# Recurrence of a two-layer block: inverses as plain products, level masks applied once per chunk

## The reference, cut to what matters

```
w = -softplus(-(w0 + tanh(wd) @ w2)) - 0.5 ; decay = exp(-exp(w))
a = sigmoid(a0 + ad @ a2)
kk = k * k_k, normed per head ; k = k * (1 + (a - 1) * k_a)
def step(state, (r, w, k, v, kk, a)):
    sa = state @ -kk
    state = state * w + outer(sa, kk * a) + outer(v, k)
    y = state @ r
```

## Time and profile before

| | |
|---|---|
| Median of 3 runs | 3220.7 us (3216.71 to 3222.69) |
| Span of the profiled execution | 3217.7 us; the page gives no other time of its own for it |
| Mean granted TensorE clock | 0.942 of full speed |
| Busy over the span | PE 88%, weight loads 71%, DVE 53%, ACT 30%, POOL 21% |

### The profile page before, as it was taken

The page is one execution under the profiler, slowest core; times in us unless marked ns, Lnnn a source line. Parts: engine busy times, 40 slices in busy tenths (PEclk is TensorE's granted clock), DMA queues, the critical chain, the costliest instruction groups (busy, mean ns, idle before and its releaser), DMA issues.

```text
span 3217.7 us, 49963 instructions
## 1 busy us (share of the span) xinstructions
PE 2847.2 (88%) x20746; PEld 2294.3 (71%) x20746; DVE 1695.8 (53%) x3047; ACT 978.0 (30%) x1832; POOL 676.8 (21%) x531
## 2 busy tenths in 40 slices
PE   7998878699999999869999977887878899999877
PEld 6776667588888888757788846777756678766655
DVE  3425565544444444576455227778745432377744
ACT  3214444311111111454221121222144222145552
POOL 2113233211101011063111102223202211122113
PEclk9998999899999999989999977989889899999988
DMA  3111032011111111113111200000032201111042
GB/s 99 50 54 45 14 100 73 25 59 46 46 49 50 46 53 40 46 53 105 53 34 46 76 21 2 3 29 3 3 99 79 87 32 35 34 40 37 30 127 95
DMA packets 200322, 162.45 MB, mean 50 GB/s; under 512 B 5232, under 2 KB 173850, under 8 KB 199586
## 3 DMA queue, kind: packets, MB, share of 16 engines
q1 hardware_dynamic: 200098, 159.26, 15.9%
HBM read 137.19 MB, written 22.05 MB: 49 GB/s over the span
## 4 chain that ended last, share of the span: by engine, by line
PE 72%; DVE 12%; ACT 6%; issue 5%; POOL 3%; DMA 2%; SPq 0%; DVEq 0%; ACTq 0%; POOLq 0%
PE ps L725 15%; PE ps L727 14%; PE ps L726 14%; PE ps L2291 7%; PE ps L1843 3%; PE ps L1767 2%; PE ps L1469 2%; PE ps L1471 1%; PE ps L1470 1%; ACT r L685 1%; PE ps L1834 1%; PE ps L777 1%; DVE r L690 1%; PE ps L779 1%; PE ps L778 1%
## 5 line engine op out<-in xcount | busy, mean ns | idle before, releaser
L725 PE MATMUL ps<-r,r 128*128 128x512 f32 (+1 forms) x2304 | 938.0, 407 | 96.8 <-DVE r L690 56.0
L726 PE MATMUL ps<-r,r 128*128 128x512 f32 (+1 forms) x2304 | 908.2, 394 | 0.0
L727 PE MATMUL ps<-r,r 128*128 128x512 f32 (+1 forms) x2304 | 907.7, 394 | 0.0
L725 PEld LDWEIGHTS ps<-r,r 128*128 128x128 f32 x2304 | 442.2, 192 | 229.6 <-DVE r L690 64.9
L671 POOL TENSOR_TENSOR sb<-sb 128x1024 f32<-128x1024 f32 x138 | 275.8, 2004 | 1301.8 <-DMA sb<-in_w_ffn_up 483.6
L726 PEld LDWEIGHTS ps<-r,r 128*128 128x128 f32 x2304 | 442.6, 192 | 93.7 <-issue 7.8
L727 PEld LDWEIGHTS ps<-r,r 128*128 128x128 f32 x2304 | 441.0, 191 | 94.0
L690 DVE TENSOR_TENSOR r<-sb,r 128x1024 fp32r<-128x1024 f32 x198 | 268.9, 1365 | 234.4 <-ACT r L685 234.1
L2291 PE MATMUL ps<-sb 64*64 64x64 f32 (+2 forms) x8832 | 298.6, 228 | 81.6 <-issue 47.8
L2291 PEld LDWEIGHTS ps<-sb 64*64 64x64 f32 (+1 forms) x8832 | 283.5, 138 | 106.7 <-issue 81.3
L685 ACT CAST r<-sb 128x1024 fp32r<-128x1024 f32 x198 | 204.9, 1043 | 215.9 <-POOL sb L671 215.8
(11 more groups left out here) (272 smaller groups left out, 3622.9 us busy)
## 6 DMA issues: line engine op xcount, KB each, us to landing
sb<-in_w_out SPq DMA_DIRECT2D x36, 512.0 KB, 4.1
sb<-in_a_w_in SPq DMA_DIRECT2D x29, 512.0 KB, 4.0
sb<-in_w_ffn_gate SPq DMA_DIRECT2D x22, 512.0 KB, 3.8
sb<-in_w_ffn_up SPq DMA_DIRECT2D x22, 512.0 KB, 3.9
sb<-in_w_ffn_down SPq DMA_DIRECT2D x22, 512.0 KB, 3.4
sb<-in_w_in SPq DMA_DIRECT2D x17, 512.0 KB, 4.1
sb<-in_x SPq DMA_DIRECT2D x16, 512.0 KB, 5.5
xs<-sb SPq DMA_DIRECT2D x4, 2048.0 KB, 9.7
```

What stands on the lines that cost most here:

```text
L725: pe.matmul(self.out, w.hi[:, q, self.cols], hi, start=(q == 0), stop=False)
L726: pe.matmul(self.out, w.hi[:, q, self.cols], lo, start=False, stop=False)
L727: ins = pe.matmul(self.out, w.lo[:, q, self.cols], hi, start=False, stop=(q == w.nk - 1))
```

## The change

The masks of the six levels become f16 constants, and DVE cuts L, copied to f16 by ACT, into its six levels once per chunk (`split_levels`). A level's W is then a plain product, and the sum with X becomes part of the products, since the identity is added to W by a further product in PSUM. What was a mask or a sum on DVE becomes a copy out of PSUM, half of them on ACT. `low`, `zi` and POOL's part go; the last correction is added in PSUM and ACT copies the result. The low-rank weights lie in one tile, w on the upper 64 rows and a on the lower, and their products alternate between both. The sigmoid's scaling moves into the constants of E: L2387 takes half of k_a, L2390 becomes (rate + 1) x kk, and L2400 a product with -0.5 in the same operation; L2322 goes. The order of a period is a new one, and the first three, partly empty periods take the place of the list ahead. The diff, cut:

```diff
@@ -160,8 +160,8 @@
-        self.level = [self.const(CH) for _ in range(6)]
-        self.level0t = self.const(CH)
+        self.masks16 = self.const(6 * CH // 2).bitcast(F16).rearrange("p (a b) -> p a b", a=6)
+        self.eye16 = self.const(CH // 2).bitcast(F16)
...
+    PERIOD = "S A S A L S A L S P P A B A P B P E B E A B B E A B E"
-        out = [("L", 0)] * 4 + [("E", 0)] * 4 + [("P", 0)] * 4 + [("E", 1)] * 4 + [("I", 0)] * 2 + [("L", 2)] * 4
-        out += [step for _ in range(4) for step in (("P", 1), ("I", 0))]
-        out += [step for _ in range(4) for step in (("I", 0), ("E", 2), ("I", 1))] + [("I", 0)] + [("I", 1)] + [("I", 0)] + [("I", 1)]
-        for m in range(NCH):
+        out = []
+        for m in range(-3, NCH):
             chunk = {"S": m, "A": m + 1, "P": m + 2, "B": m + 2, "E": m + 3, "L": m + 3}
-            for c in "S A S L A L L S L A S P P B E B E P P B A B B A E B A E".split():
-                if chunk[c] < NCH and (c != "L" or chunk[c] % 2 == 0):
+            for c in self.PERIOD.split():
+                if 0 <= chunk[c] < NCH and (c != "L" or chunk[c] % 2 == 0):
...
-                    ins = pe.matmul(self.bank(b + p // n, n, w)[o, p % n, :], lhs[o, p], rhs[o, p], start=(j == 0),
+                    ins = pe.matmul(self.bank(b + p // n, n, w)[o, p % n, :], lhs[o, p], rhs[o, p], start=(j == 0 and not onto and not (keep and p)),
...
     def low_rank_pe(self, pe, m):
         k, s = self.k, self.s
-        for dst, weights in (("tw", self.w2), ("ta", self.a2)):
-            for half, b in ((0, 0), (1, 1)):
-                pe.wait_ge(*self.freed(b))
-                for p in range(3):
+        for half in range(2):
+            pe.wait_ge(*self.freed(0))
+            pe.wait_ge(*self.freed(1))
+            for p in range(3):
+                for dst, b, o in (("tw", 0, slice(0, LORA)), ("ta", 1, slice(LORA, P))):
                     q = 3 * half + p
-                    ins = pe.matmul(self.bank(b, 3, 2 * CH)[:, p, :], weights[:, q * P:(q + 1) * P],
-                                    self.lora[:, m * CH:(m + 2) * CH], start=True, stop=True)
-                ins.then_inc(*s.low_rank.up((dst, m, half)))
-                k.free[b] = ("biased_" + dst, (m, half))
-                yield
...
                 dve.tensor_tensor(to[:, pairs], self.bank(b, 3, 2 * CH), over_tokens(bias[:, pairs], 2 * CH),
                                   ALU.add).then_inc(*s["biased_" + dst].up((m, half)))
-                if dst == "ta":
-                    dve.wait_ge(*s.tanh.at((dst, m, half)))
-                    dve.tensor_scalar(to[:, pairs], to[:, pairs], 0.5, 0.5, ALU.mult, ALU.add).then_inc(*s.rate.up((m, half)))
-                yield
...
-        b = 4 + 2 * (m % 2)
-        pe.wait_ge(*self.freed(b))
-        self.heads(pe, b, BT, CH, [(self.ar_e[:, :, 0, :], self.bb)]).then_inc(*s.p_low.up(m))
-        k.free[b] = ("low", m)
...
-        dve.wait_ge(*s.p_low.at(m))
-        dve.tensor_tensor(self.low[i], self.bank(4 + 2 * i), over_pairs(k.low), ALU.mult).then_inc(*s.low.up(m))
-        dve.wait_ge(*s.low.at(m))
-        dve.tensor_tensor(self.z[i], self.low[i], over_pairs(k.level[0]), ALU.mult).then_inc(*s.step_dve.up(("z", m)))
-        dve.wait_ge(*s.step_dve.at(("z", m)))
-        dve.tensor_tensor(self.x16[i], self.z[i], over_pairs(k.eye), ALU.add).then_inc(*s.inv_x.up((m, 0)))
+        dve.wait_ge(*s.inv_l.at(m))
+        self.split_levels(dve, m, 0, 1)
         dve.wait_ge(*s.p_ak.at(m))
         dve.tensor_tensor(self.ak[i][:, 0:3, :], self.bank(2, 3, 2 * CH), self.m3, ALU.mult)
         dve.tensor_tensor(self.ak[i][:, 3:6, :], self.bank(3, 3, 2 * CH), self.m3, ALU.mult).then_inc(*s.ak.up(m))
-        yield
-        yield
-        yield
-        yield
+        self.split_levels(dve, m, 1, 6)
+
+    def split_levels(self, dve, m, first, end):
+
+        shape = (P, end - first, BT, CH)
+        of_pair = self.l16.unsqueeze(1).broadcast_to(shape)
+        mask = self.k.masks16[:, first:end].unsqueeze(2).broadcast_to(shape)
+        dve.tensor_tensor(self.levels16[m % 2][:, first:end], of_pair, mask, ALU.mult).then_inc(*self.s.levels.up((m, first)))
...
-        if m > 1:
-            act.wait_ge(*s.inv.at(m - 2))
-        act.copy(self.l16[i], self.lr[i][:, :, 0:CH]).then_inc(*s.inv_l.up(m))
+        if m:
+            act.wait_ge(*s.levels.at((m - 1, 1)))
+        act.copy(self.l16, self.lr[i][:, :, 0:CH]).then_inc(*s.inv_l.up(m))
...
-        x16, xt16, w16 = self.x16[i], self.xt16[i], self.w16[i]
+        x16, xt16, w16, eyes = self.x16[i], self.xt16[i], self.w16[i], over_pairs(k.eye16)
+        level = [self.levels16[i][:, j] for j in range(6)]
+        pe.wait_ge(*s.levels.at((m, 0)))
+        pe.wait_ge(*self.freed(b))
+        self.heads(pe, b, BT, CH, [(level[0], eyes), (eyes, eyes)]).then_inc(*s.i_x.up((m, 0)))
+        pe.wait_ge(*self.freed(bt))
+        self.heads(pe, bt, BT, CH, [(eyes, level[0]), (eyes, eyes)]).then_inc(*s.i_xt.up((m, 0)))
+        k.free[b], k.free[bt] = ("inv_x", (m, 0)), ("inv_xt", (m, 0))
+        yield
         for lev in range(1, 6):
             if lev == 1:
-                pe.wait_ge(*s.inv_l.at(m))
+                pe.wait_ge(*s.levels.at((m, 1)))
             pe.wait_ge(*s.inv_x.at((m, lev - 1)))
             pe.wait_ge(*self.freed(b))
-            self.heads(pe, b, BT, CH, [(self.l16[i], x16)]).then_inc(*s.i_w.up((m, lev)))
+            self.heads(pe, b, BT, CH, [(level[lev], x16), (eyes, eyes)]).then_inc(*s.i_w.up((m, lev)))
             k.free[b] = ("inv_w", (m, lev))
             yield
             pe.wait_ge(*self.freed(bt))
             pe.wait_ge(*s.inv_w.at((m, lev)))
-            if lev == 1:
-                pe.wait_ge(*s.inv_xt0.at(m))
-            else:
-                pe.wait_ge(*s.inv_xt.at((m, lev - 1)))
+            pe.wait_ge(*s.inv_xt.at((m, lev - 1)))
             self.heads(pe, b, BT, CH, [(xt16, w16)]).then_inc(*s.i_x.up((m, lev)))
-            self.heads(pe, bt, BT, CH, [(w16, xt16)]).then_inc(*s.i_xt.up((m, lev)))
+            self.heads(pe, bt, BT, CH, [(w16, xt16)], keep=lev == 5).then_inc(*s.i_xt.up((m, lev)))
             k.free[b], k.free[bt] = ("inv_x", (m, lev)), ("inv_xt", (m, lev))
             yield
         pe.wait_ge(*self.freed(b))
-        pe.wait_ge(*s.inv_z.at(m))
-        self.heads(pe, b, BT, CH, [(self.low[i], self.z[i])]).then_inc(*s.i_rest.up(m))
+        pe.wait_ge(*s.inv_x.at((m, 5)))
+        self.heads(pe, b, BT, CH, [(self.lr[i][:, :, 0:CH], self.z[i]), (eyes, eyes)]).then_inc(*s.i_rest.up(m))
         k.free[b] = ("inv_rest", m)
         yield
-        pe.wait_ge(*self.freed(bt))
+        pe.wait_ge(*s.inv_xt.at((m, 5)))
         pe.wait_ge(*s.inv_rest.at(m))
-        self.heads(pe, bt, BT, CH, [(x16, self.r16[i])]).then_inc(*s.i_fix.up(m))
+        self.heads(pe, bt, BT, CH, [(self.r16[i], xt16)], onto=True).then_inc(*s.i_fix.up(m))
         k.free[bt] = ("inv", m)
...
-        k, s, i = self.k, self.s, m % 2
+        s, i = self.s, m % 2
         b, bt = 4 + 2 * i, 5 + 2 * i
-        x16, xt16, w16 = self.x16[i], self.xt16[i], self.w16[i]
+        dve.wait_ge(*s.i_x.at((m, 0)))
+        if m > 1:
+            dve.wait_ge(*s.i_fix.at(m - 2))
+        dve.tensor_copy(self.x16[i], self.bank(b)).then_inc(*s.inv_x.up((m, 0)))
+        yield
         for lev in range(1, 6):
-            dve.wait_ge(*s.i_w.at((m, lev)))
-            dve.tensor_tensor(w16, self.bank(b), over_pairs(k.level[lev]), ALU.mult).then_inc(*s.inv_w.up((m, lev)))
             yield
             dve.wait_ge(*s.i_x.at((m, lev)))
-            dve.tensor_tensor(x16, x16, self.bank(b), ALU.add).then_inc(*s.inv_x.up((m, lev)))
-            dve.wait_ge(*s.i_xt.at((m, lev)))
-            dve.tensor_tensor(xt16, xt16, self.bank(bt), ALU.add).then_inc(*s.inv_xt.up((m, lev)))
+            dve.tensor_copy(self.z[i] if lev == 5 else self.x16[i], self.bank(b)).then_inc(*s.inv_x.up((m, lev)))
             yield
         dve.wait_ge(*s.i_rest.at(m))
-        dve.wait_ge(*s.inv_zi.at(m))
-        dve.tensor_tensor(self.r16[i], self.bank(b), self.zi[i], ALU.subtract).then_inc(*s.inv_rest.up(m))
-        yield
-        dve.wait_ge(*s.i_fix.at(m))
-        if m > 1:
-            dve.wait_ge(*s.s_y.at(m - 2))
-        dve.tensor_tensor(self.xt[i], self.z[i], self.bank(bt), ALU.add).then_inc(*s.inv.up(m))
+        dve.tensor_tensor(self.r16[i], self.bank(b), self.z[i], ALU.subtract).then_inc(*s.inv_rest.up(m))
+        yield
         yield
...
-        for _ in range(10):
+        b, bt = 4 + 2 * i, 5 + 2 * i
+        act.wait_ge(*s.i_xt.at((m, 0)))
+        act.copy(self.xt16[i], self.bank(bt)).then_inc(*s.inv_xt.up((m, 0)))
+        yield
+        for lev in range(1, 6):
+            act.wait_ge(*s.i_w.at((m, lev)))
+            act.copy(self.w16[i], self.bank(b)).then_inc(*s.inv_w.up((m, lev)))
             yield
-        act.wait_ge(*s.inv_xt.at((m, 5)))
-        act.copy(self.z[i], self.xt16[i]).then_inc(*s.inv_z.up(m))
-        yield
-        yield
```

(76 more changed lines are left out.)

24 lines of the change are left out of this document (11 added, 13 removed).

## The result

The kernel after takes **3174.3 us** (median of 4 runs, 3172.24 to 3181.79) where the kernel before takes 3221.1: a ratio of 0.9861 [0.9847, 0.9875], 46.8 us less. The forecast was 3158. The profiled execution of after is its longest, 3181.79 us, and it reaches the recurrence late: the recurrence's first matmuls (L2253 in before, L2255 in after) start at 1905.1 us where before has 1895.2. So I compare stretches that begin there. From that point to the last state update it takes 414.3 us, and 460.4 before: 46.1 us, the whole difference of the medians.

What follows compares the result with a forecast made beforehand. DVE was taken to bound each chunk's second half, PE's products with ACT copies the first. Twelve periods 43 us, last three 6, start 12 and setup 1.8 made 62.8 us less: 3158 us, range 3134 to 3191.

Steps and rivals of the forecast that it cites:

- Start: Stretch ahead of the first state update: partly empty periods replace the old list, 12 us less, bounds 4 and 16.
- Last three: The last three periods, 60.4 us, hold no new products in part: 2 us less each, 6 in all.
- Setup: DVE's two memsets ahead of the w2 and a2 transfers, for which PE waits 7.49 us, go: 1.8 us less.
- (a): The 12 periods from 1987.9 to 2295.2 us: each falls from 25.6 to 22.0 us, 43 us in all.
- The first half: State matmuls of a chunk, PE products with ACT copies between: 8.1 us, 9.5 with low-rank part, mean 8.8 (9.3 before).
- signs of being wrong: PE idle naming ACT's w or xt copies, a split above 2 us, PEclk under 0.8, first half over 9 us.
- the walk: One period stepped through with operation durations and engine hops: first half mean 8.8 us, second 13.2, period 22.0.
- DVE's sum: DVE's work per chunk: 11.9 us removed, copies and splits added, 20.2 to 13.1 us; about 105 us in eight chunks.
- ACT's queue: w and xt queue on ACT and the split takes 2.2 us: period 23.8, time 3181 us. Chance 0.17.
- Unpaired low-rank products: Low-rank products do not run side by side: 1.3 us per two chunks, 10 in all, 3168 us. Chance 0.12.
- The slower clock: PE's granted clock at 0.69 through the whole recurrence: period 29 us, time 3242 us. Chance 0.03.
- New waits that take all: New waits in the period make it 25 us: 13 us less at most, or 0, about 3217. Chance 0.04.

Runs made afterwards that it cites:

- e7: The kernel after with the last three elementwise pieces (E1, E2, E3) moved from the second half into the next period's first half: 3176.2 us, ratio 0.9871.
- e9: The kernel after with each identity product of twelve matmuls, one per head, made by one wide matmul issued first: 3160.0 us, ratio 0.9820.
- e4: The kernel after with the level masks in f32 instead of f16: 3183.0 us, ratio 0.9879.
- e3: The kernel before with its low-rank products as pairs on separate halves of the rows, all else as before: 3220.1 us, ratio 0.9993.
- e6: The kernel after with the low-rank products unpaired, those of w first and those of a behind them: 3176.4 us, ratio 0.9869.
- e11: The kernel after with wide identity matmuls, plus 99 unread small matmuls per chunk ahead of the wait for the bonus sum's input: 3238.9 us, ratio 1.0067.
- e12: The kernel after with wide identity matmuls, plus DVE's two masks of the second product put ahead of its wait for ACT's two-byte copy: 3159.2 us, ratio 0.9816.
- e5: The kernel after with the five copies of w made by DVE instead of ACT: 3204.4 us, ratio 0.9949.
- e2: The kernel before with its hand-written start replaced by partly empty periods begun three chunks early: 3214.7 us, ratio 0.9982.

## Why the prediction was right in sign, and 16 us too low

*Where the gain is.* Right. Start: forecast 12, measured 11.4 (92.6 to 81.2). Last three: forecast 6, measured 3. Setup: PE's wait of 7.49 us fell to 6.17; 1.3 of the forecast 1.8.

*(a), the twelve periods, is the step that failed:* 43 us forecast, 31.6 measured. The first half has a mean of 9.5 us (forecast 8.8, and over 9 was one of the signs of being wrong), with one of 15.2 at the gates' fetch and two L halves of 10.6 and 10.4. The second has 13.5, near the 13.2 of the walk. But that match was partly luck: the walk had DVE full in it, and e7 and the 30 us of idle on DVE show that it wasn't. What was missing, a term put at nothing, is that PE's added instructions don't only cost their 16 ns: they have to arrive. The walk charged ten new groups with 1.9 us of PE time beside other work; in truth 1536 more matmuls and as many loads (22282 against 20746), packed into shorter periods, came with 17 us more of silent stops, 12 us of them in the twelve periods. With their number taken back to before's and the same arithmetic (e9), the first half is 7.7 us and with L 9.6 to 10.4 apart from the fetch (forecast 8.1 and 9.5), the second 13.0 (13.2), the period **22.1** or, with the fetch out of the way, 21.9 (22.0), and the time 3160 (3158). So the walk gave the right length for a kernel that isn't held up by the arrival of its instructions, with DVE wrongly full in it.

*DVE's sum.* Forecast 105 us busy in eight chunks, measured 121.6. Two errors. Operations printed as 0.55 us start 0.47 apart, so taking one away frees 0.47: some 1.2 us a chunk. And the slowness of L2455 and L2457 didn't go with them, it moved to L2399 and L2400 (L2396 and L2397 in before; 0.669 and 0.549 us there, 0.899 and 1.305 after) and L2403; see the last section. This time was covered.

*The rivals.* ACT's queue: refuted, ACT's copies come at 0.48 us, and the split took 1.15 us; with 2.15 (e4) the period would have been 23.7, near that rival's 23.8. Unpaired low-rank products: they pair, but e3 and e6 price this at 0 to 2 us, not 10; I had charged PE time as if no cover stood beside it. The slower clock: the reverse, 0.98 instead of 0.91. New waits that take all: the period is 22.98, not 25. The new order as such was nowhere priced in the forecast; it was worth 22 us.

## What to carry to other kernels

Look at how fast an engine with very short instructions uses them up, not only at their time: here TensorE's came in packets for 256 of them, 3.3 us apart at best. 99 identity matmuls fewer per chunk, for the same TensorE time, gave 14 us; as many put back at 32 ns or more each (e11) brought no stop. To find such a wait, compare the idle stretches that no semaphore ends with the packets of the instruction queue. Fold identities of separate heads into one wide matmul issued first, and let the products add to it. Once an engine that was full (DVE before) has lost a quarter of its work, the chain of products and copies takes over, and PE time, a covered wait or work moved off DVE's busy half (e6, e7, e12) buys nothing; a copy moved off DVE that stands in the chain (e5) still does.
